# Back-to-back transposes of a step's two probability tiles in a hybrid attention and short-convolution layer

## The reference

```python
s_c = einsum('bgqrd,bcgd->bgqrc', qb, k_c) * scale      # compressed blocks
o_cmp = einsum('bgqrc,bcgd->bgqrd', masked_softmax(s_c, ...), v_c)
s_s = einsum('bgqrd,bgqnld->bgqrnl', qb, k_g) * scale   # selected blocks (here: all of them, causal)
o_slc = einsum('bgqrm,bgqmd->bgqrd', masked_softmax(s_s, ...), v_g)
s_w = einsum('bgqrd,bkgd->bgqrk', qb, k_wb) * scale     # window of 512
o_win = einsum('bgqrk,bkgd->bgqrd', masked_softmax(s_w, ...), v_wb)
o_nsa = (g0 * o_cmp + g1 * o_slc + g2 * o_win) * silu(nsa_z)
o_conv = cv_b * conv3(cv_c * cv_h) * silu(cv_z)
out = x + concat([o_nsa, o_conv]) @ w_out
```

## Time and profile before

| what | us |
|---|---|
| median of 3 runs | 640.86 |
| lowest and highest run | 640.74, 641.78 |
| the profiled execution, its own time | 641.97 |
| its span from the first to the last instruction | 640.2 |

### The profile page before, as it was taken

How to read it: one execution, slowest core, us unless ns; L and a number is a source line. 1 busy time by engine, 2 the same in 40 slices (tenths; PEclk the granted TensorE clock), 3 DMA queues, 4 the chain that set the end, 5 groups by cost and what they waited for, 6 DMA issues and landing times.

```text
span 640.2 us, 10218 instructions
## 1 busy us (share of the span) xinstructions
PE 630.6 (99%) x3449; PEld 530.0 (83%) x3449; DVE 487.7 (76%) x1165; ACT 381.2 (60%) x888; POOL 206.4 (32%) x220
## 2 busy tenths in 40 slices
PE   9999999999999999999999999999999999999997
PEld 6889998888888888888887888877788888887876
DVE  4955979997745854787789867897888879888862
ACT  6764457664354444556666656668866666666651
POOL 2543204343333323423224222348642221312210
PEclk9999999999999999999999999999999999999999
DMA  8523111212111111101111010123211111011111
GB/s 306 177 58 117 30 38 39 62 33 82 34 50 35 50 34 33 49 18 34 34 34 34 17 34 17 41 91 130 100 52 56 45 33 67 34 34 50 50 33 67
DMA packets 20211, 37.33 MB, mean 58 GB/s; under 512 B 2880, under 2 KB 4288, under 8 KB 20160
## 3 DMA queue, kind: packets, MB, share of 16 engines
q1 hardware_dynamic: 20016, 36.68, 18.3%
q10 hardware_dynamic: 144, 0.00, 0.0%
HBM read 32.48 MB, written 4.19 MB: 57 GB/s over the span
## 4 chain that ended last, share of the span: by engine, by line
PE 80%; DVE 14%; ACT 2%; issue 2%; POOL 1%; DMA 1%; SPq 0%; DVEq 0%; ACTq 0%
PE pf L1494 10%; PE pf L1495 10%; PE pf L1496 10%; PE tp L1808 5%; PE sc L1648 4%; PE sc L1647 4%; PE po L1786 4%; PE po L1787 4%; PE sc L1494 4%; PE sc L1495 3%; PE sc L1496 3%; PE pj L1495 3%; PE pj L1494 3%; PE pj L1496 3%; DVE sc L1387 2%
## 5 line engine op out<-in xcount | busy, mean ns | idle before, releaser
L1387 DVE CUSTOM_DVE_ANT_0 sc<-sc,maskb 128x64 f32<-128x64 f32 (+8 forms) x192 | 102.7, 563 | 40.9 <-PE sc L1648 40.3
L974 ACT CAST pth<-tp 128x512 fp32r<-128x512 f32 x132 | 77.6, 588 | 85.0 <-PE tp L1808 84.8
L1415 DVE TENSOR_TENSOR ptl<-tp,pth 128x512 fp32r<-128x512 f32 x132 | 91.0, 689 | 23.7 <-ACT pth L974 23.3
L692 POOL TENSOR_SCALAR qp<-qp,precip,gate 128x64 f32<-128x64 f32 x64 | 43.5, 680 | 181.4 <-DVE precip L1377 181.3
L650 POOL TENSOR_TENSOR fl<-fraw,fh 128x512 fp32r<-128x512 f32 x40 | 54.2, 1354 | 90.3 <-ACT fh L812 90.3
L1494 PE MATMUL pf<-hh,fh 128*128 128x512 f32 x200 | 80.1, 401 | 0.0
L1495 PE MATMUL pf<-hl,fh 128*128 128x512 f32 x200 | 78.4, 392 | 0.0
L1496 PE MATMUL pf<-hh,fl 128*128 128x512 f32 x200 | 78.2, 391 | 0.0
L641 POOL TENSOR_TENSOR wl<-qp,wh 128x512 fp32r<-128x512 f32 (+1 forms) x33 | 49.5, 1522 | 86.4 <-ACT wh L732 82.6
L1808 PEld LDWEIGHTS tp<-idr,qpr 128*128 128x128 f32 x560 | 62.5, 140 | 11.8 <-issue 2.0
L1808 PE MATMUL tp<-idr,qpr 128*128 128x128 f32 x560 | 65.7, 238 | 0.8 <-POOL qp L692 0.6
(11 more groups left out here) (258 smaller groups left out, 1568.9 us busy)
## 6 DMA issues: line engine op xcount, KB each, us to landing
fraw<-in_wside SPq DMA_DIRECT2D x40, 256.0 KB, 2.6
qp<-in_wpack SPq DMA_DIRECT2D x28, 256.0 KB, 3.3
xo<-in_x SPq DMA_DIRECT2D x16, 256.0 KB, 2.8
out<-xo SPq DMA_DIRECT2D x16, 256.0 KB, 2.1
wor<-in_wout SPq DMA_DIRECT2D x12, 256.0 KB, 2.8
mixc<-in_xcm SPq DMA_DIRECT2D x4, 512.0 KB, 7.3
xlow<-in_xcm SPq DMA_DIRECT2D x3, 512.0 KB, 6.6
qp<-in_wpack SPq DMA_DIRECT2D x5, 224.0 KB, 2.6
```

Of the source, the lines that this page charges most:

```text
L974: nc.scalar.copy(pth[ptn % 2][:, :], tp[tpn % 2][:, :]).then_inc(pth_ready, 1)
L1387: return V.tensor_tensor_reduce(row, row, mask, -1.0, -NEG, ALU.add, ALU.min, most)
L1415: V.tensor_tensor(ptl[ptn % 2][:, :], tp[tpn % 2][:, :], pth[ptn % 2][:, :].bitcast(F32), ALU.subtract).then_inc(tp_read, 1)
```

## The change

PE: in a two-tile step both tiles are transposed one right behind the other at the head of the step, then comes the carry's value product, then the side parts of group 0, then the scores where a unit begins, then A's value product. One-tile steps keep their order. `pending` becomes a list, so that two tiles can be owed at once.

ACT: the cast of B moves ahead of the side work of group 0. DVE's order is unchanged.

```diff
@@ ACT, step k
+                for kind, _ in turned[1:]:
+                    prob_hi(kind)
                 for f in side_ends(k, 0):
                     if f < NF:
                         side(f)
-                for kind, _ in turned[1:]:
-                    prob_hi(kind)
@@ PE
-            pending = None
+            pending = []
             def flush():
-                if pending is None:
+                if not pending:
                     return
-                n, (kind, j), pt, first = pending
-                pending = None
+                n, (kind, j), pt, first = pending.pop(0)
...
-            def turn(n, kind, j, between=None):
+            def turn(n, kind, j):
...
-                if between is not None:
-                    scores(between)
-                flush()
-                pending = (n, (kind, j), ptn, n % 2 == 0 and j == 0)
+                pending.append((n, (kind, j), ptn, n % 2 == 0 and j == 0))
                 ptn += 1
@@ PE, step k
-                    turn(n, *turned[0])
+                    for t in turned:
+                        turn(n, *t)
+                    if len(pending) > len(turned):
+                        flush()
...
-                for c, t in enumerate(turned[1:]):
-                    turn(n, *t, k + 1 if first_of_unit and c == 0 else None)
+                if len(turned) > 1:
+                    if first_of_unit:
+                        scores(k + 1)
+                    flush()
```

More of the change, by code:

```diff
@@ L1764, in _ @@
             scores(0)
-            pending = None
+            pending = []
             def flush():
-                nonlocal pending
-                if pending is None:
+                if not pending:
                     return
-                n, (kind, j), pt, first = pending
-                pending = None
+                n, (kind, j), pt, first = pending.pop(0)
                 i, g = UNITS[n // 2]
@@ L1792, in _ @@
             tp_of = {}
-            def turn(n, kind, j, between=None):
-                nonlocal tpn, ptn, pending
+            def turn(n, kind, j):
+                nonlocal tpn, ptn
                 i, g = UNITS[n // 2]
```

## The result

The changed kernel takes 642.88 us (median of 14 runs, 641.93 to 644.3), the kernel before 641.0 us beside it (14 runs, 640.19 to 642.41). The ratio is 1.0028, 95% interval 1.0021 to 1.0036: slower by 1.8 us, where 640.6 us and a range up to 642.0 had been predicted. The profiled execution of the changed kernel took 643.38 us.

What follows compares the result with a forecast made beforehand. The prediction took PE to bound the kernel, busy 630.6 of 640.2 us. Gains of 1.59 less losses of 1.25 gave 0.3 us net, 640.6 us forecast; own range 639.6 to 642.1, 8 in 10 638.7 to 642.0.

Steps and rivals of the forecast that it cites:

- the two signs of being wrong: PE's waits for DVE's subtraction fall by over 2 us in all, or grow in steps where a side tile ends.
- Spacing on PE: A's value product, now behind a side product, takes 0.02 us less in 21 steps: 0.42 us gained.
- B's cast ahead of the side work: Step 68: ACT casts B before the side copy, so PE's value product starts earlier: 0.32 us gained.
- B's transpose earlier: Steps where DVE or ACT idled for B: 0.25 us gained in step 128, 0.35 in step 90.
- Side tiles behind B's transposes: Step 132: B's transposes fill the new side tile's wait for its bank: 0.25 us gained.
- The new wait: Step 119: B's transposes wait until DVE has read the unit's queries: 0.61 us lost.
- Side tiles that end in a two-tile step: DVE's work on finished side tiles starts 0.30 us later: 0.30 lost in step 127, 0.24 in 74, 90 and 106.
- Unit boundaries: Four steps where the carry ends a unit: its product, 0.30 us later, releases the po copy: 0.1 us lost.
- Rival 1: DVE regains most idle time; all 5.4 us of waits at value products go: 635.1 us, half 638; chance 0.29.
- Rival 2: DVE's late start on finished side tiles costs 0.30 us in all 12 steps, 3.6 us: 643.7 us; chance 0.17.
- Rival 3: Nothing changes, everything that moves is hidden: 640.9 us; chance 0.53 together with the forecast.
- Rival 4: Clock halved over eight transposes together, 1.2 instead of 0.6 us in 38 steps: 664 us; chance 0.01.

Runs made afterwards that it cites:

- experiment 3: Changed kernel with the former PE order in steps 74 and 76 alone: 642.24 us, ratio 1.0007 to the kernel before.
- experiment 5: Changed kernel with POOL's subtraction for weight halves 34 and 35 on 1 of 512 columns: 642.26 us (1.0003); kernel before with the same edit: 642.16 us (1.0000).
- experiment 8: Experiment 7's kernel with the new PE order also in step 82: 640.98 us, ratio 0.9986; or also in step 74 instead: 640.76 us, ratio 0.9984.
- experiment 6: Changed kernel with the former PE order in steps 74, 76, 84 and 119: 641.31 us, ratio 0.9986 to the kernel before.
- experiment 7: Changed kernel with the new PE order only in steps 68, 86, 90, 92, 94, 128 and 132: 640.40 us, ratio 0.9965 to the kernel before.
- experiment 9: Experiment 7's kernel with the new PE order also in 19 two-tile steps, 96 to 126 without 119: 640.18 us (0.9986); or also in step 127: 639.92 us (0.9982).
- experiment 4: Changed kernel with the former PE order throughout, leaving ACT's new order alone: 641.16 us, ratio 0.9996 to the kernel before.
- experiment 2: Changed kernel with the former PE order in step 119 alone: 642.30 us, ratio 1.0013 to the kernel before.

## Why the prediction was wrong, point by point

**The step that failed** is the sentence that in most other two-tile steps an earlier cast changes nothing. It looked at DVE's queue behind the cast and not at ACT's: behind B's cast stand weight casts, and POOL's subtractions start from those. "No DMA, SP or POOL instruction is moved" holds for their order and not for their time. With the new order in steps 74, 76 and 82 POOL's subtractions came 0.6 to 1.1 us earlier against the scores beside them, and in front of a DVE operation that then took 0.8 to 1.0 us longer. The prediction put this at nothing. It costs 1.33 us in steps 76 and 77 (experiments 3, 5, 8) and 0.85 us in step 84 (experiment 8, the means read from its rows). In the changed kernel 0.21 us of that came back in step 86; with step 84 in the former order hardly any did (0.05 and 0.04 in experiments 6 and 8). With the new order in seven other steps alone the change gains (experiment 7). Of the two signs of being wrong that the prediction named, neither came: PE's waits for the subtraction grew, but in steps 76, 77 and 84, in which no side tile ends.

**Spacing on PE** had the wrong sign. The 0.02 us gained at A's value product is there (0.22 after 0.25). But the row of four transposes was taken to hold for eight as well: eight take 0.64 us, not 0.60. Net it is 0.33 / 19 = 0.02 us lost a step (experiment 9, what the unit boundaries cost included) where 0.02 was to be gained; if the other steps are like these, some 0.7 us over the 38, where 0.42 us of gain stood in the sum. The Trainium skill, page "TensorE: Matmul & The Clock Gate", section "Back-to-back issue gap", gives an isolated gap of 56 ns for a product of 128 columns and about 81 ns for a stream of loads and products. The mean of the run of eight comes near the second, 0.64 / 8 = 80 ns, against 0.30 / 4 = 75 in the short run. But in both the spacing isn't even: in step 112 the first two transposes start 0.06 us apart and all further ones 0.08 to 0.09, so the short run has the larger share of near ones.

**B's cast ahead of the side work**: 0.32 predicted, 0.41 measured, of which only 0.19 come by ACT's order alone (experiment 4); the rest comes by PE's, so the number fits better than the mechanism.

**B's transpose earlier**: steps 90 to 95 gained 0.74 us, where 0.35 was taken for step 90 and 0.4 was the bound. It came in steps 91 (0.22), 92 (0.32) and 94 (0.28); the prediction counted nothing for 92 and 94, and which of the three reordered steps gives how much was not separated. ACT's 1.15 us of idle time in step 90 is gone. The head of step 129 lost its wait as predicted:

```profile
618.28 0.29 PE L1806 MATMUL tp<-idr,qpr 128*128 128x128 f32 x2
618.40 0.41 PE L1784 MATMUL po<-ptl,val 128*64 128x512 f32 x1
...
625.82 0.39 PE L1785 MATMUL po<-pth,val 128*128 128x512 f32 x1
626.05 0.40 PE L1494 MATMUL pf<-woh,msh 128*128 128x512 f32 x1
```

That is 0.12 us after 0.40, a gain of 0.28 for 0.25. **Side tiles behind B's transposes**, the lower pair, step 132: 0.23 after 0.40; with the side product behind it 0.25 us (0.46 after 0.71), as predicted.

**The new wait** in step 119: 0.61 predicted, 0.66 measured, 0.63 of it by that step's order (experiment 2).

**Side tiles that end in a two-tile step**: step 127 cost 0.33 us for 0.30 (experiment 9). For 74, 90 and 106 another 0.24 was taken; 90 and 106 show 0.03 each, and what 74 lost it lost by the collision. **Unit boundaries**: steps 101, 109, 117 and 125 lose 0.05 to 0.06 us each, 0.02 of it the spacing, so 0.13 for 0.10 (step 110 loses 0.07 more, 118 gives 0.06 back).

**The rivals.** Rival 1 is excluded: DVE did get half of its 23.3 us back, and PE's waits grew. Rival 2's figure, 643.7, is near the result, but that is chance: of the twelve steps in which DVE takes out a side tile only 127 shows a loss of 0.3 us by it. Rival 3 is excluded too: the interval of the ratio, 1.0021 to 1.0036, does not hold 1. Rival 4 is excluded by the clock, 0.999 over the span with eight transposes in a row, which took 0.64 us and not 1.2. All four rivals asked what is late; none asked what becomes early.

Left open: the median lost 1.8 us and the profiled execution 1.4; the 0.4 us between them lie within the interval, and no run settles them. The 0.26 us that step 82 gained in that one trace may be part of it.

## What to carry to other kernels

When work on one engine is moved forward, follow that engine's queue to what it releases on the others, and look there at what runs beside it now. An earlier start can put two operations side by side that exclude each other, and the loss then appears one or two steps behind the edit. An order that helps where an engine really waits is better taken step by step than everywhere: seven of 38 steps gave 0.35% (0.21 to 0.48), all 38 cost 0.28% (0.21 to 0.36).

## What the runs showed of the hardware

Which of DVE and POOL goes first can differ at the same start times. In step 79 POOL's scaling of the compressed probabilities (L692) starts 0.06 to 0.07 us behind DVE's L1383 and 0.46 to 0.47 us ahead of DVE's L1361 in all 14 traces, and yet there are two outcomes. POOL and DVE before, then of experiment 4:

```profile
420.28 0.73 POOL L692 TENSOR_SCALAR qp<-qp,precip,gate 128x64 f32<-128x64 f32 x1 [1.39 <-DVE precip L1377]
420.98 1.73 POOL L650 TENSOR_TENSOR fl<-fraw,fh 128x512 fp32r<-128x512 f32 x1
...
420.22 0.61 DVE L1383 TENSOR_SCALAR qp<-qp,precip,gate 128x640 f32<-128x640 f32 x1
420.75 0.80 DVE L1361 SCALAR_TENSOR_TENSOR mixc<-ub,prm,mixc 128x512 f32<-128x512 f32 x1
421.47 1.78 DVE L1352 SCALAR_TENSOR_TENSOR mixc<-th,mixc 128x512 f32<-128x512 f32 x1
```

```profile
420.49 1.32 POOL L692 TENSOR_SCALAR qp<-qp,precip,gate 128x64 f32<-128x64 f32 x1 [1.39 <-DVE precip L1377]
421.78 1.73 POOL L650 TENSOR_TENSOR fl<-fraw,fh 128x512 fp32r<-128x512 f32 x1
...
420.43 0.61 DVE L1383 TENSOR_SCALAR qp<-qp,precip,gate 128x640 f32<-128x640 f32 x1
420.96 0.75 DVE L1361 SCALAR_TENSOR_TENSOR mixc<-ub,prm,mixc 128x512 f32<-128x512 f32 x1
421.62 0.73 DVE L1352 SCALAR_TENSOR_TENSOR mixc<-th,mixc 128x512 f32<-128x512 f32 x1
```

Where POOL's small operation ends only behind L1361 (1.32 us), its next one comes too late to hold up L1352, and PE gains 1.07 to 1.09 us in steps 79 and 80. That was so in 3 of the 14 traces (experiments 4, 6 and the 19 steps of 9). The edits don't decide it: four of the 14 kernels have the same order up to this step (experiment 7, step 82 of 8, and both of 9), and one of the four went the other way. What decides it is not shown, and L692 starts ahead of L1361 in both outcomes, so the start in the profile doesn't tell who goes first here. Part of the spread between executions of one kernel may be this (each kernel was traced once), and a span of a single profile is not a measure of an edit here.

The collisions are not new with the change. In the loop of the kernel before, L1361 at 326.8 us and L1383 at 218.4, 274.4, 443.6 and 531.0, for example, take 0.75 to 1.05 us longer than the shortest of their shape, and each starts 0.06 to 0.28 us behind a POOL subtraction. The change added three such and took away the one at 531.0. What those before the change cost PE is not shown.

The other surprise is the price of what follows transposes. Behind a run of them, a product with 64 columns of weights takes 0.25 us (median of 108 in the trace before) and one with 128 columns 0.30 (median of 14), where 0.22 to 0.23 is undisturbed.
